# First block: the gate's limit as a two-input instruction, its second products on four row groups, the low-rank weights split ahead of the squares

## The reference

```python
proj = h @ w_in[l]
(g_q, g_k, g_v, g_r, g_lr_f, g_lr_b, s_q, s_k, s_v, gate_a, gate_b) = jnp.split(proj, split_at, axis=-1)
...
def log_gate(lr, up, bias):
    z = lr.astype(f32) @ up.astype(f32) + bias.astype(f32)
    lg = jnp.maximum(jax.nn.log_sigmoid(z) / GLA_GATE_NORMALIZER, GLA_LOG_GATE_MIN)
    return heads(lg, GLA_DK)
```

## Time and profile before

| | |
|---|---|
| time, median of 3 runs | 1898.42 us (1898.35 to 1899.20) |
| profiled execution, its own time | 1899.83 us |
| its span in the profile | 1897.9 us |
| PE busy | 1875.3 us (99%) |
| DVE, ACT, POOL busy | 1523.3 us (80%), 1240.1 us (65%), 403.3 us (21%) |
| chain of work that ended last, by engine | PE 93%, DVE 3%, POOL 1%, ACT 1%, issue 1% |

### The profile page before, as it was taken

How to read it: one execution, slowest core, us unless ns; L and a number is a source line. 1 busy time by engine, 2 the same in 40 slices (tenths; PEclk the granted TensorE clock), 3 DMA queues, 4 the chain that set the end, 5 groups by cost and what they waited for, 6 DMA issues and landing times.

```text
span 1897.9 us, 26327 instructions
## 1 busy us (share of the span) xinstructions
PE 1875.3 (99%) x9450; PEld 1578.4 (83%) x9450; DVE 1523.3 (80%) x1649; ACT 1240.1 (65%) x1484; POOL 403.3 (21%) x206
## 2 busy tenths in 40 slices
PE   9999999999999999999999999999999999999997
PEld 6888888888898888878888888888888888888886
DVE  6745367777576887697699999999999999999997
ACT  6654444444644444464488888888888888888876
POOL 6856870001824000282450000000000000000000
PEclk9999999999999999999999999999999999999999
DMA  9534556665434676534599999999999999999994
GB/s 284 170 119 134 178 186 218 224 221 172 142 122 133 206 242 221 163 120 134 176 383 395 391 380 376 386 397 368 389 365 388 396 365 388 366 387 396 370 395 188
DMA packets 251397, 523.68 MB, mean 276 GB/s; under 512 B 9944, under 2 KB 58720, under 8 KB 251184
## 3 DMA queue, kind: packets, MB, share of 16 engines
q1 hardware_dynamic: 243408, 504.00, 74.2%
q10 hardware_dynamic: 5680, 11.61, 1.7%
q0 software_dynamic: 2224, 6.95, 1.1%
HBM read 507.19 MB, written 15.34 MB: 275 GB/s over the span
## 4 chain that ended last, share of the span: by engine, by line
PE 93%; DVE 3%; POOL 1%; ACT 1%; issue 1%; DMA 0%; SPq 0%; DVEq 0%; ACTq 0%
PE bank L726 25%; PE bank L728 24%; PE bank L727 24%; PE bank L1081 6%; PE bank L1084 3%; PE bank L1160 2%; POOL w_lo_sb L655 1%; PE bank L849 1%; PE bank L1345 1%; PE bank L822 1%; PE bank L828 1%; DMA arena<-in_w_in 0%; PE bank L990 0%; PE bank L967 0%; DVE arena L2050 0%
## 5 line engine op out<-in xcount | busy, mean ns | idle before, releaser
L1971 DVE TENSOR_TENSOR w_lo_sb<-arena,w_hi_sb 128x1024 fp32r<-128x1024 f32 x672 | 807.8, 1223 | 73.8 <-ACT w_hi_sb L1499 43.6
L1499 ACT ACTIVATE w_hi_sb<-arena 128x1024 fp32r<-128x1024 f32 x672 | 711.2, 1062 | 168.7 <-PE bank L728 168.0
L726 PE MATMUL bank<-w_hi_sb,left_sb 128*128 128x512 f32 (+1 forms) x1400 | 553.4, 395 | 2.8 <-POOL w_lo_sb L655 2.8
L728 PE MATMUL bank<-w_hi_sb,left_sb 128*128 128x512 f32 (+1 forms) x1400 | 542.3, 387 | 0.0
L727 PE MATMUL bank<-w_lo_sb,left_sb 128*128 128x512 f32 (+1 forms) x1400 | 541.5, 387 | 0.0
L1519 ACT ACTIVATE w_hi_sb<-arena 128x1024 fp32r<-128x1024 f32 (+1 forms) x269 | 278.2, 1052 | 299.8 <-PE bank L728 220.8
L655 POOL TENSOR_TENSOR w_lo_sb<-arena,w_hi_sb 128x1024 fp32r<-128x1024 f32 (+1 forms) x134 | 341.6, 2569 | 552.0 <-ACT w_hi_sb L1519 551.2
L726 PEld LDWEIGHTS bank<-w_hi_sb,left_sb 128*128 128x128 f32 x1400 | 263.1, 188 | 61.1 <-POOL w_lo_sb L655 7.6
L728 PEld LDWEIGHTS bank<-w_hi_sb,left_sb 128*128 128x128 f32 x1400 | 262.9, 188 | 54.9
L727 PEld LDWEIGHTS bank<-w_lo_sb,left_sb 128*128 128x128 f32 x1400 | 263.4, 188 | 50.9 <-issue 0.7
L726 PE MATMUL bank<-w_hi_sb,hid_hi_sb 128*128 128x512 f32 x656 | 257.3, 392 | 0.1
(11 more groups left out here) (356 smaller groups left out, 1687.5 us busy)
## 6 DMA issues: line engine op xcount, KB each, us to landing
arena<-in_moe_w_gate SPq DMA_DIRECT2D x112, 1024.0 KB, 7.9
arena<-in_moe_w_up SPq DMA_DIRECT2D x112, 1024.0 KB, 8.0
arena<-in_moe_w_down SPq DMA_DIRECT2D x112, 1024.0 KB, 7.7
arena<-in_w_in SPq DMA_DIRECT2D x45, 1024.0 KB, 5.1
arena<-in_w_ffn_in SPq DMA_DIRECT2D x22, 1024.0 KB, 5.1
arena<-in_w_out SPq DMA_DIRECT2D x12, 1024.0 KB, 5.1
arena<-in_w_ffn_out SPq DMA_DIRECT2D x11, 1024.0 KB, 4.8
arena<-in_dense_w_gate SPq DMA_DIRECT2D x11, 1024.0 KB, 5.4
```

Source lines behind the costliest of these rows:

```text
L726: pe.matmul(out, still[0], moving[0], start=start, stop=False)
L728: return pe.matmul(out, still[1], moving[0], start=False, stop=stop)
L1499: act.activation(expert_buffer(w_hi_sb, j), expert_piece(j % MOE_SUBS), ACT.Copy) \
L1971: dve.tensor_tensor(expert_buffer(w_lo_sb, j), expert_piece(j % MOE_SUBS), expert_buffer(w_hi_sb, j).bitcast(F32), ALU.subtract) \
```

## The change

**The limit** (L2050) becomes a `scalar_tensor_tensor` whose two tensor inputs are the same tile, both operations a maximum; its result is the same.

**The second products** of both directions are made in one place, behind piece 6. To that end the low-rank weights are repeated four times along the columns when piece 4 is split (its parts are now 128 x 1024 instead of 128 x 256), so that the low-rank products come out four times, on partitions 0 to 31, 32 to 63, 64 to 95 and 96 to 127. The up-weights lie in 128 partitions x 512: each group of 32 rows holds the 16 rows of one direction, each direction twice, the rest is zero. The four matmuls (two directions, two halves of the tokens) each use one group of 32 rows of the array. GpSimd therefore loads the up-weights four times instead of twice, 9 loads instead of 7 are counted by `gates_landed`, and the tile that it clears is 128 x 512 instead of 32 x 1024.

**The split of piece 4** moves ahead of the squares on ScalarE.

```diff
+        REPEATS = P // (2 * GLA_RANK)
+
+        def split_buffer(store, j, w):
+
+            k, n = w.shape[1:]
+            if j != span["lr"][0]:
+                return buffer(store, j, k, n)
+            return buffer(store, j, k, REPEATS * n).rearrange("p k (r n) -> p k r n", r=REPEATS)
+
+        def repeated(j, w):
+            return over(w, 2, REPEATS) if j == span["lr"][0] else w
...
-        g_up = room(16640, 1024)[0:2 * GLA_RANK, :].rearrange("p (a n) -> p a n", a=2)
-        g_lrT = room(17664, TOKENS)[0:2 * GLA_RANK, :]
+        g_up, g_lrT = room(16640, 512), room(17664, TOKENS)
...
+        GATES_LANDED = 16 * (4 + 2 + 2 + 1)
...
             for a, d in enumerate(("fwd", "bwd")):
-                rows(g_up[a * GLA_RANK:(a + 1) * GLA_RANK, a, :], A[f"gla_gate_up_{d}"][0], "gates_landed")
+                for t in range(T):
+                    at = (2 * a + t) * 2 * GLA_RANK + a * GLA_RANK
+                    rows(g_up[at:at + GLA_RANK, :], A[f"gla_gate_up_{d}"][0], "gates_landed")
...
-                w = [buffer(a, first, KD, 2 * GLA_RANK) for a in (w_hi_sb, w_lo_sb)]
+                w = [buffer(a, first, KD, P) for a in (w_hi_sb, w_lo_sb)]
                 b = gemm_bank[(gemm_at["sq1"] + 1) % 4]
                 for k in range(KD):
-                    mm = three_passes(b[0:2 * GLA_RANK, 0:TOKENS], [a[:, k, :] for a in w],
+                    mm = three_passes(b[:, 0:TOKENS], [a[:, k, :] for a in w],
                                       (left_hi[:, k, :], left_lo[:, k, :]), k == 0, k == KD - 1)
...
-            def gate_up(a):
-
-                pe.wait_ge(sem("gates_landed"), 16 * 7)
+            def gate_up():
+
+                pe.wait_ge(sem("gates_landed"), GATES_LANDED)
                 pe.wait_ge(sem("g_lrT_ready"), 1)
-                for t in range(T):
-                    pe.matmul(pair("z", 2 * a + t)[:, :], g_lrT[:, t * P:(t + 1) * P], g_up[:, a, :],
-                              start=True, stop=True).then_inc(sem("pair_full"), 1)
+                for n in range(2 * T):
+                    rows, tokens = slice(2 * GLA_RANK * n, 2 * GLA_RANK * (n + 1)), slice(n % T * P, (n % T + 1) * P)
+                    pe.matmul(pair("z", n)[:, :], g_lrT[rows, tokens], g_up[rows, :], start=True, stop=True) \
+                        .then_inc(sem("pair_full"), 1)
...
-            gemm("sq1", between={1: lambda: gate_up(0), 3: lambda: gate_up(1)})
+            gemm("sq1", between={1: gate_up})
...
-                        act.activation(buffer(w_hi_sb, j, *w.shape[1:]), w, ACT.Copy).then_inc(sem("w_hi_ready"), 1)
+                        act.activation(split_buffer(w_hi_sb, j, w), repeated(j, w), ACT.Copy) \
+                            .then_inc(sem("w_hi_ready"), 1)
...
             first_hi(3)
+            split_to(span["lr"][1])
             squares(range(2 * T), [(f"x_landed{q // T}", 16) for q in range(2 * T)], "ss_f0")
...
-            dve.tensor_copy(g_lrT, gemm_bank[(gemm_at["sq1"] + 1) % 4][0:2 * GLA_RANK, 0:TOKENS]) \
+            dve.tensor_copy(g_lrT, gemm_bank[(gemm_at["sq1"] + 1) % 4][:, 0:TOKENS]) \
                 .then_inc(sem("g_lrT_ready"), 1)
...
-                dve.tensor_scalar(g_lg[:, a, :, :], g_lg[:, a, :, :], LEAST_GATE, None, ALU.max).then_inc(sem("z_ready"), 1)
+                gate = g_lg[:, a, :, :]
+                dve.scalar_tensor_tensor(gate, gate, LEAST_GATE, gate, ALU.max, ALU.max).then_inc(sem("z_ready"), 1)
```

6 lines of the change are left out of this document (3 added, 3 removed).

## The result

The changed kernel takes 1902.27 us (median of 22 runs, 1900.03 to 1903.68), the kernel before 1898.66 us (22 runs, 1897.64 to 1899.52). The ratio is 1.0017, 95% interval [1.0011, 1.0023]: slower by 0.1 to 0.2%, inside what the prediction called no measurable change, but outside its range of 1896.6 to 1901.2 us. The profiled execution took 1902.14 us, its span is 1900.2 us.

The account below looks back on a forecast made before the run. TensorE's own work plus its few waits bound the kernel. Terms +1.0 (queue), -1.9 (second pair), -1.0 (waits at 45.95 and 52.10), +2.1 (pieces 14 to 16), +0.8 (piece 21) gave +1.0: 1899.4 us, range 1896.6 to 1901.2.

Parts of the forecast that it names:

- The base of the sum: Terms of +1.0 us added to the profiled execution (1899.83), giving 1900.8, less its 1.41 us over the median: 1899.4.
- The two loads: Two more DMAs on GpSimd's queue move everything behind, up to its first low part (piece 7), back: +1.0 us.
- The low-rank piece: Wider split ahead of the squares moves PE's resumption from 24.96 to 25.6: +0.66 us, within the queue's +1.0.
- The limit: First two-input limit on the Vector engine: asked for at 32.7, runs from 34.5 to 35.7; before, it ended at 38.69.
- A wait for one GpSimd instruction instead of three: The two-input limit on the Vector engine never waits for more than one GpSimd piece; piece 11 no longer holds PE.
- the second rival: The two-input limit starves like the old one, until GpSimd's four pieces are through: 1900.8 to 1901.9 us, chance 0.15.
- Second products: Four products behind piece 6 take 0.95 to 3.8 us, near the lower bound; the pair behind piece 8 disappears: -1.9 us.
- What is late next: Pieces 9 to 21: rope turns make the second limit, then splits and low parts late: +2.1 (pieces 14 to 16), +0.8 (21).
- The turns: Limits and rope steps run between GpSimd's pieces; low parts of pieces 9 to 13 done at 37.9, 41.2, 44.0, 46.8, 50.2.
- the waits at pieces 14, 15 and 21: PE stands for GpSimd's late low parts: 1.3 us at piece 14, 0.8 at 15, some 0.8 more at 21.

Follow-up runs that it names:

- after_look: The changed kernel profiled once more, nothing changed: 1899.88 us (1 run).
- two_loads: The kernel before with each up-weight load issued a second time on GpSimd's queue, into rows nothing reads: 1900.25 us, ratio 1.0008.
- gap_first: The kernel before with one added wait, GpSimd starting piece 7 only when PE has used piece 6: 1899.64 us, ratio 1.0001.
- two_by_sync: The changed kernel with the two added up-weight loads issued by SyncE instead of GpSimd: 1901.36 us, ratio 1.0016.
- fixed_sync: The changed kernel, GpSimd's piece 7 behind table products, 9 behind first limit, router and mask loads behind 17, added up-weight loads on SyncE: 1899.28 us, ratio 1.0002.
- fixed_before: The kernel before, GpSimd's piece 7 behind the table products, piece 9 behind the first limit, router and mask loads behind piece 17: 1898.35 us, ratio 0.9998.
- limit_alone: The kernel before with the two-input form of the limit and nothing else: 1899.92 us, ratio 1.0004.
- products_apart: The changed kernel with the second products in two places again, two behind piece 6 and two behind piece 8: 1902.22 us, ratio 1.0016.
- split_back: The changed kernel with the split of the wide low-rank piece behind the squares again: 1900.88 us, ratio 1.0011.
- ordered_after: The changed kernel with one-input limit, early router load, GpSimd's piece 9 behind the first limit, splits of pieces 14 and 21 earlier: 1901.23 us, ratio 1.0010.

## Why the prediction was wrong

Three steps failed: the two-input limit waits like the old one, the two loads cost more than their place in the queue, and the sum was set against the median of the kernel before as if its profiled execution differed from it by a constant. What follows takes the terms one by one.

**The base of the sum.** The prediction added +1.0 us to the profiled execution and then took off 1.41 us, its distance to the median, as if that lay around the kernel. It was the course itself: the starved limit and the wait at piece 11 that it set out to price. An execution with the limit let in starts piece 24 at 88.47, the profiled one at 90.57. For the course that it described, a limit let in, the sum was even too high: after_look, at 1899.88, took 0.05 us more than the profiled execution of before, against +1.0 forecast. The forecast is 2.9 us under the measured median: 1.4 are this base, 1.3 that the profiled execution of the changed kernel was 2.3 us over that of before and not 1.0, 0.1 lies between that execution and its median. The changed kernel's median, 1902.27, lies at its caught execution (1902.14; the other took 1899.88), that of the kernel before, 1898.66, between its two (1897.72 and 1899.83). Of the profiles in which nothing orders the limit, five of the eight of the changed kernel and its variants show a caught instruction, and two of the five of the kernel before and its variants. How common either course is isn't shown run by run.

**The two loads.** +1.0 us was right for GpSimd's place in the queue (piece 7 at 32.48 and 32.13, forecast 32.2). What the step left out is that other loads come later with them: the tables landed at 25.9 in two_loads and at 25.5 and 27.0 in the two profiles of the changed kernel, against 24.4 before. The load of the weights of pieces 9 and 10 was issued at 18.3 to 18.8 in every profile, but these were split from 32.9 to 34.9 in the ten profiles with the two loads on GpSimd's queue, and from 31.6 to 33.1 in nine of the ten without (34.51 in gap_first). That shrank GpSimd's lead. The price is 1.3 us by two_loads, 0.9 by two_by_sync and 1.0 by fixed_sync, each inside its interval: some 1 us, not settled.

**The low-rank piece.** 25.6 was forecast for PE's resumption; 25.65 and 25.77 came where the two loads are off the queue, 25.93 and 26.28 in the changed kernel. The term held to 0.3 us (in 26.28 the later start is another 0.3); that it would come on top of GpSimd's 1.0 us, by the products and the limit that follow it, was missed. No run prices that alone: what fixed_sync still costs over fixed_before, 0.93 us, is left for it and the products, and with these intervals that isn't settled.

**The limit.** "A wait for one GpSimd instruction instead of three" was wrong (limit_alone 7.09 us). Rows 4 had shown turns for the rope's steps, but these came after GpSimd had stood still; the row to go by was the old limit's, the only instruction met ahead of that. This was the second rival, given 0.15, and its 1900.8 to 1901.9 us came nearest; its place was wrong, since in the changed kernel's profile the starved instruction stood ahead of the limit.

**Second products.** Right: 1.14 us near the lower bound, and the second pair gone. The 1.9 us became waiting: from 20 to 95 us PE stood 4.9 and 3.4 us in the two profiles of the changed kernel, 1.7 us and none in those of before, and products_apart puts half of the work back at the same time (1902.22).

**What is late next.** The turns were right to within 0.1 us at pieces 9 and 10 (37.9 and 41.2, measured 37.84 and 41.18), then 0.6 to 1.1 us short. Of the waits at pieces 14, 15 and 21 (1.3, 0.8 and 0.8 forecast) the changed kernel shows only 0.46 us at piece 21, in after_look; fixed_sync, where the limit and the weights come as early as the sum supposed, shows all three, 1.01, 0.37 and 0.93.

**Not in the sum: the clock.** Where PE stood 1.98 us or more ahead of piece 11 (six profiles), the granted clock fell to 1.2 GHz behind it; after 1.42 us in the kernel before it did not. By the spacing of pieces 11 to 13, 6.9 to 7.2 us against 5.44 at the full clock, that is 1.5 to 1.8 us on top of the wait (8.38 us in split_back, the longest wait). In two_loads it fell at piece 7, to 0.75 over 31.2 to 38, where PE had stood 0.81 us; in ordered_after it did not, after 1.43 us ahead of piece 9. These rows give no rule for it.

**The sum of it.** By medians: 3.6 us, of which 2.0 remain with the queues in order, and 1.6 go with the order. The two profiles without a caught instruction (2.1 us apart) bear out the 2.0; the 1.6 are the remainder. How the 2.0 divide between the two loads and the low-rank piece stays open: the medians give 1.0 and 0.9, with intervals as wide as these shares.

## What to carry to other kernels

Work taken from the engine that sets the time pays only while its suppliers keep their lead: count the lead at each piece ahead of the saving, and price every added instruction on a supplier's queue, small loads too, by what it moves behind it. Where one profile lies off the median by as much as the change is meant to give, take a second one ahead of the forecast: the course that is to be mended may not be the usual one. Two engines that block each other are better ordered by a semaphore than left to meet: fixed_before held its runs within 1.3 us, where those of the kernel before beside it spread over 2.4, at a median that can't be told from theirs.
